# Both parts of a projection block behind one step of the recurrent heads, and none behind every second step

## The chip, the cores and the metric

The kernel runs on one core of one Trainium2 chip. The metric is the device time of one execution in microseconds; of the kernel before, three executions are given, and one more was profiled.

## The reference

A one-layer encoder trunk runs on two token groups with shared weights, a sample group of 1024 tokens and a prompt group of 512, both 1024 wide, in float32:

```python
h = rms_norm(x, norm_mix_g)
proj = h @ w_in                                  # 8 blocks of 512 columns
aq, ak, av, hq, hff, hfb, hi, hg = split(proj)
att = diff_attention(aq, ak, av)                 # 4 heads, softmax with a distance bias
q, v = silu(hq), hi                              # 4 recurrent heads, 128 x 128
f = lb + (1 - lb) * sigmoid(hff or hfb)          # a gate for each direction
o = hgrn2_scan(q, 1 - f, v, log f)  forwards  +  the same backwards
hgo = rms_norm(o, hg_norm_g) * silu(hg)
x = x + concat(att, hgo) @ w_out
x = x + expert_choice_ffn(rms_norm(x, norm_ffn_g))   # 16 experts
return rms_norm(x, final_norm_g)
```

Within the scan, token t reads token s through the product of all gates between them. The kernel works that out over levels of doubling length instead of token by token.

## The kernel before

The mixer (the first 940 us or so) runs the four recurrent heads of the sample, its four attention heads, and then the same for the prompt. The experts follow. The change lies in the recurrent heads.

**A recurrent head** (function `hgrn`, L843) takes tokens in blocks of 512: `NB` is 2 for the sample and 1 for the prompt. Its steps stand in the list `slots` (L884 to L893): `start`; `v_rows` for each block; for each block eight `level` steps and a `diag`; for each direction `k_rows` and `state` for each block; then `o`, `squares`, `mean`, `norm`, `mix`. Step names with numbers are written here as in the list: `("level", b, k)` is level k of block b, `("state", d, b)` is direction d, block b.

- A `level` step on TensorE is 64 small matmuls (L994; 32 at L1000 for level 6, 16 at L1005 for level 7) that read q and k of both directions. On VectorE it multiplies q and k by products of gates, three instructions a direction (L1134, L1135, L1137; one, L1127, at level 0). VectorE's update waits until TensorE has read (`level_read`, L1166), and TensorE's next level waits for the update (`updated`, L986).
- `diag` has nothing for TensorE. VectorE masks and reduces four banks of scores (L1177, L1182), and the next block's level 0, or `k_rows` and `state`, wait until the bank that they write has been read (`x_uses`, L899).
- `k_rows` is four transposes on TensorE (L1016) and a copy on ScalarE (L1105). `state` is four products on TensorE (L1025), then a chain of short additions on VectorE (L1195, L1198). `k_rows` (1,0) takes the bank that `state` (0,1) filled, and `o` (L1045) needs all states.

**The next head's projection** is computed beside the present head's steps (class `Projection`, L510). It has ten units (five outputs V, Q, two gates and G, each in two halves of the contraction), `NB` blocks for each unit, and each block in `CUTS` = 2 parts of six matmuls with 512 columns (L599 to L601). The method `piece` (L605) turns the number of a part into steps: the part itself, `("unit", u, b, part)`; ahead of a unit's first part the `split` of unit u + 1 (ScalarE L568 rounds the weights, VectorE L572 makes the remainder); behind the last part of an output its `land` (ScalarE L1075, and for Q and G VectorE L1150). A unit's first part waits for its own split's remainder (`lo`, L580).

**The order** is written out, not found by a scheduler. `beside` (L617) walks through the head's steps, counts them (all but `squares` and `mean`), and puts behind each step so many parts that their number keeps in proportion; `lead` parts, `NB` of them, go in at once. Every engine runs this one list in its own queue, skipping what isn't its own, and an instruction that waits holds up all behind it on that engine. The list is `stages[1]`. It is run for three heads of each group: a loop of two (`heads`, L735) and the one after it, in which the prompt has some extra steps for the output weights. The fourth head of each group runs without a projection beside it (`stages[2]`), mixed with the first attention projection. `beside` also makes `stages[0]`, which has a single step.

SyncE loads the raw weights (L556) into a ring of five slots. A load waits for the split five units earlier (L555).

Of the kernel before, what the change touches and what calls it, by code (L numbers as in the profile page):

```python
# [29 lines left out]
CUTS = 2  # L30
# [585 lines left out]

def beside(slots, proj, lead=0):  # L617


    pieces = CUTS * proj.units * proj.NB  # L620
    out, done, passed = [("split", 0)], 0, 0
    counted = lambda step: step[0] not in ("squares", "mean")
    total = sum(map(counted, slots))
    for step in slots:
        out.append(step)
        passed += counted(step)
        upto = lead + (pieces - lead) * passed // total
        for n in range(done, upto):
            out += proj.piece(n)
        done = upto  # L630
    return out
# [211 lines left out]
def hgrn(sem, g, T, w_in, masks_in, consts, banks, mem, after, rows):  # L843
# [47 lines left out]
    if NB == 2:  # L891
        slots += [("o", 1), ("norm", 0), ("squares", 1), ("mean", 1), ("mix", 0)]
    slots += [("norm", NB - 1), ("mix", NB - 1)]  # L893
    stages = beside([("none",)], proj), beside(slots, proj, NB), slots
    in_order = [s for s in slots if s[0] == "state"]
    nth = lambda step: in_order.index(step)
# [700 lines left out]
def project_out(sem, xs, w_out, g_ffn, w_router, consts, banks, mem, aff, aff_last, shares, index, index_cols, gate_cols, h2_dram, y_dram, rows, before_h, before):  # L1597
# [255 lines left out]
    def vector(dve):  # L1853
# [74 lines left out]
        return body  # L1928

    return Heads(None, (early, beside, tiles), (early_loads, late_loads), tensor, scalar, vector, gpsimd, {})  # L1930


def experts(nc, ctx, w_gate, w_up, w_down, g_final, ident, minus_half, psum, banks, index_cols, gate_cols, h2_dram, y_dram, out_p, out_s):
# [13 lines left out]
    with ExitStack() as c:  # L1947
# [74 lines left out]
        def pair_steps(i, late, last):  # L2022

            out = []
            after = {Q - 1: ("gate", 0), Q: ("silu", 0), 2 * Q - 1: ("up", 0), 2 * Q: ("high", 0), 2 * Q + 1: ("low", 0),
                     3 * Q - 1: ("gate", 1), 3 * Q: ("silu", 1), 4 * Q - 1: ("up", 1), 4 * Q: ("high", 1), 4 * Q + 1: ("low", 1)}
            for p in range(2):
                for n in range(UNITS):
                    ahead = n + PARTS - 1
                    if ahead < UNITS:  # L2030
                        out.append(("split", i, p, ahead))
                    elif not (last and p == 1):
                        out.append(("split", *next_of(i, p), ahead - UNITS))
                    out.append(("unit", i, p, n))
                    if n in after:
                        out.append((after[n][0], i, p, after[n][1]))
                    if n == 4 * Q + 2 and not (last and p == 1):
                        out.append(("turn", *next_of(i, p)))
                    if late:
                        u = (2 * i + p - FIRST_LATE) * UNITS + n  # L2040
                        out += [(kind, i, p, q) for later, kind in enumerate(("square", "mean", "norm")) for q in beside(u, later)]
                out.append(("last" if last and p == 1 else "result", i, p))
            return out
# [421 lines left out]
```

How the kernel before makes its waits and increments, by code:

```python
    def step(self, dve, n):  # L156
        rows, table, column, what = self.steps[n]
        eight, places = (t[rows, column:column + TOP] for t in (self.shares, self.index))
        if n:
            dve.wait_ge(self.sem, n)
        if what == 0:
            dve.max(eight, table).then_inc(self.sem, 1)
        elif what == 1:
            dve.max_index(places, eight, table).then_inc(self.sem, 1)
        else:
            dve.match_replace(table, eight, table, -2.0).then_inc(self.sem, 1)
# [59 lines left out]
    def halves(self, pool):  # L227
        pool.memset(self.minus_half[:], -0.5).then_inc(self.halved, 1)
        pool.wait_ge(self.halved, 1)
# [9 lines left out]
    def scalar(self, act):  # L239
        act.wait_ge(self.chain, 3)
        act.activation(self.lam_exp[:], self.lam_sum[:], ACT.Exp).then_inc(self.exps, 1)
        act.activation(self.lb_e[:], self.lb_r[:], ACT.Exp).then_inc(self.exps, 1)
        act.wait_ge(self.filled, self.FILLED)
# [4 lines left out]
    def vector(self, dve):  # L248
        chain, att_g, lb, lb_e, lb_r = self.chain, self.att_g, self.lb, self.lb_e, self.lb_r
        dve.wait_ge(self.loaded, 7 * 16)
        for n in range(2):
            dve.tensor_tensor_reduce(out=self.lam_prod[:, n, :], in0=self.lam_in[:, 2 * n, :],
                                     in1=self.lam_in[:, 2 * n + 1, :], scale=1.0, scalar=0.0,
# [9 lines left out]
        dve.wait_ge(chain, 5)  # L263
        dve.tensor_tensor(lb_e[:], lb_e[:], lb_r[:], ALU.mult).then_inc(chain, 1)
        dve.wait_ge(chain, 7)
```

## Time and profile before

| | us |
|---|---|
| three executions, median (lowest, highest) | 2191.89 (2191.11, 2194.22) |
| the profiled execution | 2191.68 |
| its span, first to last instruction | 2189.9 |
| TensorE matmuls busy | 2008.1 (92%) |
| VectorE busy | 1468.9 (67%) |
| ScalarE busy | 1111.4 (51%) |
| GpSimd busy | 290.1 (13%) |

By stage, the first three sample heads lie between about 87 and 348 us, and TensorE is busy 252.69 us of those 261; the first three prompt heads lie between about 756 and 895 us, with TensorE busy 128.28 of 139.

In a timeline row the first number is the start in us from the span's start and the second how long the instruction (or a merged run of `xN` of them) took. The end of a matmul overlaps the start of the next, so the step from start to start is what one costs. PE is TensorE, DVE VectorE, ACT ScalarE. A bracket gives the idle time of the engine in front of the instruction, and who ended it.

### The profile page before, as it was taken

The page shows a single profiled execution, that of the slowest core. Times are in us where ns is not written, and L with a number is a line of the kernel's source. Part 1 is how long each engine was busy: PE and PEld are TensorE (multiplying, and loading weights), DVE is VectorE, ACT ScalarE, POOL GpSimd, SP SyncE. Part 2 cuts the span into 40 slices and gives each one's busy share as a digit, 9 for nine tenths or more (in the row PEclk, how much of TensorE's full clock was granted, in tenths as well). Part 3 has the DMA queues.
Part 4 walks back from the last instruction along what each step waited for, and adds up shares of the span by engine and source line. Part 5 has one row for each costly group of instructions (what it writes and reads, how often), then busy time and mean ns, then how long its engine had stood idle before and what let it go on. Part 6 is the DMA issues. An engine that isn't in the chain of part 4 may idle for free. (4 is left out here: it accounts for less than half of the span.)

```text
span 2189.9 us, 43441 instructions
## 1 busy us (share of the span) xinstructions
PE 2008.1 (92%) x16048; PEld 1753.0 (80%) x16048; DVE 1468.9 (67%) x2769; ACT 1111.4 (51%) x1983; POOL 290.1 (13%) x419
## 2 busy tenths in 40 slices
PE   7999998899897899798899379999999999999996
PEld 6877876777786777676788279999999999999995
DVE  5466575666666577676348857777777777778876
ACT  5322322456565523265322156767666667667774
POOL 1101101000000011100122001111111111111234
PEclk9999998999998999999999689999999999999998
DMA  5211100100002122211233088787778787778995
GB/s 180 83 31 31 35 26 16 38 20 24 19 6 82 48 59 83 64 53 53 106 114 114 36 273 260 249 258 249 259 247 262 245 260 248 255 255 301 348 323 188
DMA packets 183465, 317.82 MB, mean 145 GB/s; under 512 B 11872, under 2 KB 82016, under 8 KB 183328
## 3 DMA queue, kind: packets, MB, share of 16 engines
q1 hardware_dynamic: 169984, 281.06, 38.1%
q0 software_dynamic: 8608, 30.68, 5.6%
q10 hardware_dynamic: 4736, 4.19, 0.6%
q8 instruction: 93, 1.52, 0.3%
q14 instruction: 44, 0.36, 0.1%
HBM read 279.97 MB, written 35.91 MB: 144 GB/s over the span
## 5 line engine op out<-in xcount | busy, mean ns | idle before, releaser
L2267 DVE TENSOR_TENSOR we_lo<-raw,we_hi 128x1024 fp32r<-128x1024 f32 x384 | 466.1, 1224 | 188.8 <-ACT we_hi L2192 187.8
L2158 PE MATMUL psum<-x_parts,we_hi 128*128 128x384 f32 x2048 | 585.0, 360 | 3.1 <-DVE we_lo L2267 3.1
L2160 PE MATMUL psum<-x_parts,we_lo 128*128 128x192 f32 x2048 | 513.4, 251 | 0.0
L2192 ACT CAST we_hi<-raw 128x1024 fp32r<-128x1024 f32 x384 | 400.1, 1054 | 156.6 <-PE psum L2160 93.3
L2160 PEld LDWEIGHTS psum<-x_parts,we_lo 128*128 128x128 f32 x2048 | 392.0, 191 | 0.6
L2158 PEld LDWEIGHTS psum<-x_parts,we_hi 128*128 128x128 f32 x2048 | 385.5, 188 | 4.1 <-issue 3.5
L599 PE MATMUL psum<-hT_hi,w_hi 128*128 128x512 f32 x512 | 215.5, 421 | 0.8 <-issue 0.8
L601 PE MATMUL psum<-hT_hi,w_lo 128*128 128x512 f32 x512 | 203.6, 398 | 0.0
L600 PE MATMUL psum<-hT_lo,w_hi 128*128 128x512 f32 x512 | 202.9, 396 | 0.0
L599 PE MATMUL psum<-hP_hi,w_hi 128*128 128x512 f32 x256 | 109.5, 428 | 15.9 <-DVE w_lo L572 11.6
L601 PEld LDWEIGHTS psum<-hT_hi,w_lo 128*128 128x128 f32 x512 | 97.8, 191 | 22.0
L599 PEld LDWEIGHTS psum<-hT_hi,w_hi 128*128 128x128 f32 x512 | 98.0, 191 | 20.2 <-issue 1.2
L600 PEld LDWEIGHTS psum<-hT_lo,w_hi 128*128 128x128 f32 x512 | 98.4, 192 | 16.6
L572 DVE TENSOR_TENSOR w_lo<-w_raw,w_hi 128x512 fp32r<-128x512 f32 x96 | 68.6, 715 | 52.3 <-ACT w_hi L568 50.1
L601 PE MATMUL psum<-hP_hi,w_lo 128*128 128x512 f32 x256 | 102.8, 401 | 0.0
L600 PE MATMUL psum<-hP_lo,w_hi 128*128 128x512 f32 x256 | 102.7, 401 | 0.0
L2174 PE MATMUL psum<-we_hi,hid_parts 128*128 128x512 f32 x256 | 101.3, 396 | 0.0
L568 ACT CAST w_hi<-w_raw 128x512 fp32r<-128x512 f32 x96 | 59.1, 616 | 80.9 <-PE psum L601 80.7
L2175 PE MATMUL psum<-we_lo,hid_parts 128*128 128x512 f32 x256 | 99.8, 390 | 0.0
L2176 PE MATMUL psum<-we_hi,hid_parts 128*128 128x512 f32 x256 | 99.7, 390 | 0.0
L2178 PE MATMUL psum<-we_lo,hid_parts 128*128 128x512 f32 x256 | 99.6, 389 | 0.0
L2177 PE MATMUL psum<-we_hi,hid_parts 128*128 128x512 f32 x256 | 99.6, 389 | 0.0
(313 smaller groups left out, 3774.0 us busy)
## 6 DMA issues: line engine op xcount, KB each, us to landing
raw<-in_w_gate SPq DMA_DIRECT2D x128, 512.0 KB, 4.7
raw<-in_w_up SPq DMA_DIRECT2D x128, 512.0 KB, 6.7
raw<-in_w_down SPq DMA_DIRECT2D x128, 512.0 KB, 5.0
w_raw<-in_w_in SPq DMA_DIRECT2D x96, 256.0 KB, 2.9
y_rows<-x SPq DMA_DIRECT2D x12, 512.0 KB, 2.6
h_rows<-h SPq DMA_DIRECT2D x12, 512.0 KB, 2.9
y<-y_rows SPq DMA_DIRECT2D x12, 512.0 KB, 7.9
w_raw_s<-in_w_in SPq DMA_DIRECT2D x16, 256.0 KB, 2.9
```

What stands on the lines that cost most here:

```text
L599: pe.matmul(out[:], mem.w_hi[:, u % 2, n, :], hi, start=(k == 0), stop=False)
L600: pe.matmul(out[:], mem.w_hi[:, u % 2, n, :], lo, start=False, stop=False)
L601: mm = pe.matmul(out[:], mem.w_lo[:, u % 2, n, :], hi, start=False, stop=(k == DT - 1))
L2158: pe.matmul(out[:, 0:2 * SLOTS], w_hi[:, s, at], x_parts[p][:, k, :, :], start=(k == 0), stop=False, skip_group_check=True)
L2160: mm = pe.matmul(out[:, SLOTS:2 * SLOTS], w_lo[:, s, at], x_hi[p][:, k, :], start=False, stop=(k == DT - 1), skip_group_check=True)
L2174: pe.matmul(out[2 + h][:], a, u, start=first, stop=False)
L2175: pe.matmul(out[2 + h][:], a, v, start=False, stop=False)
L2176: pe.matmul(out[2 + h][:], b, u, start=False, stop=last)
L2177: pe.matmul(out[h][:], both, u, start=first, stop=False)
L2178: mm = pe.matmul(out[h][:], both, v, start=False, stop=last)
L2192: act.copy(w_hi[:, n % PARTS, :], raw[:, s, :]).then_inc(hi.sem, 1)
L2267: dve.tensor_tensor(w_lo[:, n % PARTS, :], raw[:, n % RAW, :], w_hi[:, n % PARTS, :].bitcast(F32), ALU.subtract).then_inc(lo.sem, 1)
```

## The change

Before parts are put behind a step, the number reached is rounded down to an even number, so that both parts of a block stand behind the same step. The last step still reaches all parts. A sample head's first step gets two parts, where it had three; a prompt head's keeps two.

```diff
 def beside(slots, proj, lead=0):
 
-
     pieces = CUTS * proj.units * proj.NB
     out, done, passed = [("split", 0)], 0, 0
     counted = lambda step: step[0] not in ("squares", "mean")
     total = sum(map(counted, slots))
     for step in slots:
         out.append(step)
         passed += counted(step)
         upto = lead + (pieces - lead) * passed // total
+        upto -= upto % CUTS
         for n in range(done, upto):
             out += proj.piece(n)
         done = upto
     return out
```

For steps that follow each other in a sample head this gives (sN is the split of unit N, u.b.p part p of block b of unit u):

```
step            before             after
level 0, 3      s3 2.0.0           -
level 0, 4      2.0.1              s3 2.0.0 2.0.1
level 0, 5      2.1.0              -
level 0, 6      2.1.1              2.1.0 2.1.1
level 0, 7      s4 3.0.0           -
diag 0          3.0.1 3.1.0        s4 3.0.0 3.0.1
level 1, 0      3.1.1 land Q       3.1.0 3.1.1 land Q
```

and in a prompt head:

```
step            before             after
level 0, 6      4.0.1              s5 4.0.0 4.0.1
level 0, 7      s6 5.0.0           -
diag 0          5.0.1 land         s6 5.0.0 5.0.1 land
k_rows 0, 0     s7 6.0.0           -
state 0, 0      6.0.1              s7 6.0.0 6.0.1
k_rows 1, 0     s8 7.0.0           -
state 1, 0      7.0.1 land         s8 7.0.0 7.0.1 land
```

## Rows read from the trace of the kernel before

**Rows 1.** Busy time by stretch: window, length, busy us of each engine, granted clock (PEclk)
```profile
core 0: us, PE busy (x) PEld busy (x) DVE busy (x) ACT busy (x) POOL busy (x), PEclk, DMA share, GB/s
87.00:174.00 87.00, 83.67 (x1215) 66.36 (x1214) 55.82 (x140) 23.05 (x57) 10.93 (x24) 1.00 0.11 33
203.00:210.00 7.00, 5.18 (x138) 3.56 (x137) 5.91 (x10) 1.10 (x2) 2.35 (x8) 0.79 0.09 27
```
**Rows 2.** Timeline of TensorE, sample head, block 0: level 3, a part, level 4
```profile
102.41 0.76 PE L994 MATMUL psum<-q,k 128*32 128x32 f32 x64
103.12 0.48 PE L599 MATMUL psum<-hT_hi,w_hi 128*128 128x512 f32 x1
...
104.69 0.76 PE L994 MATMUL psum<-q,k 128*32 128x32 f32 x64
```
**Rows 3.** Timeline of VectorE: first and last instruction of updates, level 3 and level 1
```profile
102.95 0.22 DVE L1134 TENSOR_TENSOR fup<-fup 128x64 f32<-128x64 f32 x1 [0.55 <-PE psum L994]
...
104.23 0.42 DVE L1137 TENSOR_TENSOR k<-k,fup 128x256 f32<-128x256 f32 x1
...
185.25 0.42 DVE L1134 TENSOR_TENSOR fup<-f 128x256 f32<-128x256 f32 x1 [1.02 <-PE psum L994]
...
186.94 0.42 DVE L1137 TENSOR_TENSOR k<-k,f 128x256 f32<-128x256 f32 x1
```
**Rows 4.** Timeline: a level that waited for the update, block 1, level 2
```profile
124.46 0.41 DVE L1137 TENSOR_TENSOR k<-k,f 128x256 f32<-128x256 f32 x1
124.92 0.46 PE L994 MATMUL psum<-q,k 128*32 128x32 f32 x32 [0.55 <-DVE k L1137]
125.31 0.50 PE L599 MATMUL psum<-hT_hi,w_hi 128*128 128x512 f32 x1
```
**Rows 5.** Timeline: level 7 and diagonal of block 0, three parts, level 0 of block 1
```profile
111.38 0.97 PE L1005 MATMUL psum<-q,k 128*64 128x64 f32 x16
112.28 0.50 PE L599 MATMUL psum<-hT_hi,w_hi 128*128 128x512 f32 x1
...
113.60 0.68 DVE L572 TENSOR_TENSOR w_lo<-w_raw_s,w_hi 128x512 fp32r<-128x512 f32 x1
...
116.60 0.33 PE L994 MATMUL psum<-q,k 128*32 128x32 f32 x16
...
118.65 0.55 DVE L1177 TENSOR_TENSOR table<-psum,table 128x384 f32<-128x384 f32 x1
...
119.76 0.50 PE L599 MATMUL psum<-hT_hi,w_hi 128*128 128x512 f32 x1
```
**Rows 6.** Timeline: k_rows (1,0), k_rows (1,1), state (1,0), o of the same head
```profile
148.19 1.11 DVE L1198 SCALAR_TENSOR_TENSOR state<-state,fend_f,psum 128x128 f32<-128x128 f32 x3 [2.30 <-PE psum L1025]
149.37 0.66 PE L1016 MATMUL psum<-ident,k 128*128 128x128 f32 x4
...
151.25 0.60 PE L1016 MATMUL psum<-ident,k 128*128 128x128 f32 x4
151.89 0.59 ACT L1105 COPY k_rows<-psum 128x512 f32<-128x512 f32 x1 [1.24 <-PE psum L1016]
...
155.35 1.05 PE L1025 MATMUL psum<-v_rows,k_rows 128*128 128x128 f32 x8
156.44 1.12 DVE L1198 SCALAR_TENSOR_TENSOR state<-state,fend_b,psum 128x128 f32<-128x128 f32 x3 [0.82 <-PE psum L1025]
...
157.81 0.46 PE L1045 MATMUL psum<-v_rows,at 128*128 128x128 f32 x2
```
**Rows 7.** Timeline of a prompt head: levels 5 and 6, k_rows (0,0), o
```profile
818.44 0.76 PE L994 MATMUL psum<-q_p,k_p 128*32 128x32 f32 x64
...
821.81 0.50 PE L599 MATMUL psum<-hP_hi,w_hi 128*128 128x512 f32 x1
...
827.15 0.60 PE L1016 MATMUL psum<-ident,k_p 128*128 128x128 f32 x4
...
831.72 0.68 DVE L572 TENSOR_TENSOR w_lo<-w_raw,w_hi 128x512 fp32r<-128x512 f32 x1
...
836.22 0.45 PE L1045 MATMUL psum<-v_rows,at_p 128*128 128x128 f32 x2
```

## The prediction

> **What bounds the kernel now.** I read the busy shares by stage first, then the timeline of TensorE through one recurrent head, then VectorE over the same stretch. In the first of the changed heads TensorE is busy 83.67 of 87.00 us at full clock, VectorE 55.82 and ScalarE 23.05 [rows 1]. So the head costs what TensorE issues, plus its few gaps, and the question is which gaps a new order opens.
>
> Inside the head a chain runs under that busy engine. A level's score matmuls on TensorE must read q and k before VectorE may update them, and the next level's matmuls need the update: TensorE level k, VectorE update k, TensorE level k+1. What hides the update is the projection part between two levels. A level takes 103.12 - 102.41 = 0.71 us to issue, a part with its entry and exit 104.69 - 103.12 = 1.57, so levels follow each other every 2.28 us [rows 2]. A longer group of parts costs less per part: three take 116.60 - 112.28 = 4.32, so each part beyond the first costs (4.32 - 1.57)/2 = 1.38 and two together 2.95 [rows 2, 5]. An update of both directions lasts from 102.95 to 104.23 + 0.42 = 104.65, thus 1.70 us, starting 0.54 after the level's start [rows 2, 3]; at level 1, whose products are wider, 186.94 + 0.42 - 185.25 = 2.11 [rows 3]. The signal to TensorE takes 124.92 - (124.46 + 0.41) = 0.05 us, say 0.06, and the second direction of a level then takes 125.31 - 124.92 = 0.39 [rows 4].
>
> **The change, part by part.** Nothing is added or removed; parts move. Rounding `upto` down to a whole block holds every first part back one step, where it meets its second. The 1024-token pass has 35 counted steps with 40 parts, the 512-token pass 18 with 20. Working the list out by hand: after the change no parts stand after levels 1, 3, 5 and 7 of either block, after v_rows 1, k_rows (0,0) and (1,1), state (0,1) and (1,0), o 1 and mix 0; in the 512-token pass after v_rows, levels 1, 3, 5, 7, both k_rows, and o. The list serves three heads of each pass (a loop of two and the one after it). The steps "split" and "land" move with the parts.
>
> *Level pairs, 1024 tokens.* With nothing between them, the second level's second direction can start 0.54 + 1.70 + 0.06 = 2.30 after the first level's start, ends 0.39 later, and two parts follow: 2.30 + 0.39 + 2.95 = 5.64 us for two levels and two parts, now 2 x 2.28 = 4.56. That is +1.08 each for levels 3-4 and 5-6 of both blocks: +4.3. Levels 1-2 of block 0 use the 2.11 update: +1.5.
>
> *Block 0's diagonal to level 2 of block 1.* Level 7 starts at 111.38, the masked products hold the score banks until 118.65 + 0.55 = 119.20, and parts resume at 119.76 [rows 5]; level 2's next part starts at 125.31 [rows 4] and ends at 126.88, six parts in all. After the change the split on VectorE at 113.60, which holds the diagonal back by 0.60 (its 0.68 overlaps the next), stands behind it. So banks come free 0.60 earlier, parts resume at 119.16 and two end at 122.11. Level 1's update started at 124.87 - 2.11 = 122.76 because VectorE first waited for a landing of the part just ended, 1.40 after level 1's start (119.76 + 1.60 = 121.36). The same 1.40 again gives 123.51, + 2.11 + 0.06 + 0.39 = 126.07, + 2.95 = 129.02: +2.1. It also takes 1-2 of block 1 in.
>
> *State steps.* k_rows (1,0) starts at 149.37, just after VectorE's state chain ends at 148.19 + 1.11 = 149.30; so does o 0 at 157.81, after 156.44 + 1.12 = 157.56 [rows 6]. These starts are set by VectorE and don't move when the part in front of them goes; the part is owed behind them: +1.4 each, +2.8. Between k_rows (1,1) at 151.25 and its state step ScalarE's copy must end (151.89 + 0.59 + 0.06 = 152.54, 1.29 after) where a part now covers it; then state 0.81 and two parts 2.86 make 4.95, against 155.35 - 151.25 = 4.10: +0.85 [rows 6]. The 0.81 is an estimate of the state step's issue, its row's 1.05 less the overlap of its end, and 2.86 is the pair's 2.95 less the dearer exit to a level.
>
> *Head entry, k_rows (0,0), end of head.* One part fewer stands before level 0, which waits for GpSimd's k; the part follows behind. No row here shows that margin. The norm chain at the end has as many parts around it as before. I take -0.2 for group entries saved (1.57 - 1.38 = 0.19 each); bounds -1 (five entries) and +2 (the moved part wholly exposed, and some of the norm).
>
> Sum for a 1024-token head: 1.5 + 4.3 + 2.1 + 2.8 + 0.85 - 0.2 = 11.4 us; three heads, 34.
>
> *512 tokens.* Levels 1-2 +1.5, levels 3-4 +1.1. At 5-6 the landing of Q delays the update today: level 5 starts at 818.44 and parts resume at 821.81, 3.37 later [rows 7]. That wait stays, with 2.95 behind it in place of 1.57: +1.4. The largest term is the diagonal. Split 6 moves behind it on VectorE, and unit 6 is the next one TensorE wants, after the state step. Today the split that follows the diagonal is number 7, at 831.72 to 832.40; with split 6 taken from in front, its place is 0.60 earlier, so unit 6 can start at 831.86. TensorE has finished the state step at 827.15 + 1.29 + 0.81 = 829.25, so it stands 2.6 us. Then two parts to 834.8, ScalarE's copy until 1.29 after its start (k_rows (1,0), 834.8 to 836.1), state 0.81, two parts 2.86: o starts at 839.8, now 836.22; k_rows (0,0) is at 827.15 in both [rows 7]. That is +3.6. At the end of the head split 9 now follows the norm: +0.3. Sum 1.5 + 1.1 + 1.4 + 3.6 + 0.3 - 0.1 = 7.8; three heads, 23.
>
> *Loads.* SyncE's queue keeps its order; each load waits for a split that comes at most one step later, and the ring is five slots deep. I take nothing; bounds 0 and +1 us per head.
>
> *Clock.* The granted clock was 0.79 over 203 to 210 us, in the second head, where TensorE was busy 5.18 of 7.00; over the first head's same place it stayed at 1.00 [rows 1]. That is 0.21 x 7 = 1.5 us lost after one stall. The three new 2.6 us stalls of the 512-token diagonal look like it; I take two falls, +3, with bounds 0 and +33 (below).
> The Trainium skill, "TensorE: Matmul & The Clock Gate", section "A second HAM failure mode: psum-queue depth-cycling", tells of a kernel whose short idles between groups of matmuls made the clock swing between its two levels. By that rule all the small gaps here count, not the long ones alone; the trace has it after the long gap of the diagonal and not in the first head.
>
> Total 34 + 23 + 3 = 60 us. The profiled execution took 2191.68 us (span 2189.9), the median of three runs is 2191.89, so the two can be used alike: 2191.7 + 60 = 2252 us.
>
> **Rivals.**
> *A: fewer changes of group win (faster, 2182 us).* Runs of parts fall from 31 to 20 in a 1024-token head and from 16 to 10 in a 512-token one, 51 in all; each saves 1.57 - 1.38 = 0.19 us, 9.7 us. It needs the empty steps to cost nothing: a level's update would have to be done within the level's own 0.71 us. Against it: 1.70 us [rows 3]. It decides from the point where update plus signals is under 0.9 us.
> *B: no change (2192 us).* Waits shift onto stalls that exist anyway. For it: VectorE is idle a third of the head. Against: it is idle waiting for TensorE, and TensorE has 3.3 us of gaps in 87 [rows 1].
> *C: levels pay, the rest is hidden (2221 us).* If the state and diagonal terms are absorbed, there remain 3 x (1.5 + 4.3) + 3 x (1.5 + 1.1 + 1.4) = 29 us. For it: these terms rest on an order of several engines. Against: VectorE sets those starts today [rows 6, 7].
> *D: the clock falls often (2282 us).* There are 45 new gaps (ten and five per head); if half bring the 1.5 us of the second head, +33 less the 3 counted. The skill's rule above is this case. Against: the level pairs keep TensorE busy about four fifths.
>
> **Numbers.** Forecast 0.74, A 0.02, B 0.03, C 0.11, D 0.10. The forecast's own range is 2236 to 2268 (entries, loads, sizes of waits). Taking in most of C and D gives 2220 to 2282. A change of 0.2%, about 4 us, is what a measurement of this kernel can tell from none. Faster 0.02, same 0.03, slower 0.95.
>
> **What would show it.** TensorE's idle before the matmuls of even levels should be about 1.3 us a time, released by VectorE's update of k, with none before odd levels. In the 512-token heads the first matmul of unit 6 should wait about 2.6 us for w_lo, and state steps should wait for ScalarE's k_rows. A 1024-token head should last about 98 us, a 512-token one 52 to 53. It would be wrong if TensorE's idle between two levels without parts is under 0.5 us, or if heads keep their length while another stage moves.

## The result, and the profile after

The changed kernel took 2265.11 us (median of three, 2261.26 to 2267.69) against 2191.89. The ratio is 1.0329, 95% interval 1.0314 to 1.0345. The forecast was 2252 us within 2220 to 2282. The profiled execution took 2261.26 us, span 2259.5.

First the page of the changed kernel, its busy times:

```profile
PE 2023.2 (90%) x16048; PEld 1768.3 (78%) x16048; DVE 1466.4 (65%) x2769; ACT 1110.4 (49%) x1983; POOL 292.5 (13%) x419
```

The instruction counts are those of before. TensorE is busy 15.1 us longer with the same matmuls: part of it ran at half clock. The rest of the 69.6 us that the span grew, 54.5, is time in which TensorE waits. Next the busy time of the two changed stages, from the first transpose of `v_rows` of head one to that of head four, first of the kernel before:

```profile
core 0: us, PE busy (x) PEld busy (x) DVE busy (x) ACT busy (x) POOL busy (x), PEclk, DMA share, GB/s
91.59:346.88 255.29, 247.50 (x3619) 196.79 (x3618) 163.52 (x417) 64.78 (x164) 31.15 (x71) 0.99 0.11 31
760.10:891.21 131.11, 123.12 (x1802) 96.08 (x1801) 92.09 (x224) 43.14 (x101) 15.98 (x39) 1.00 0.23 67
```

and of the changed kernel:

```profile
core 0: us, PE busy (x) PEld busy (x) DVE busy (x) ACT busy (x) POOL busy (x), PEclk, DMA share, GB/s
89.14:383.39 294.25, 253.69 (x3625) 204.57 (x3624) 163.49 (x418) 64.56 (x165) 33.45 (x72) 0.98 0.09 27
799.09:961.15 162.06, 132.90 (x1801) 104.38 (x1800) 91.21 (x224) 43.10 (x101) 15.98 (x39) 0.94 0.18 54
```

The three sample heads take 39.0 us more, the three prompt heads 31.0, the whole span 69.6. What stands ahead of them is 2.5 us shorter and the fourth sample head 2.4 longer, which cancel; no other stage differs by more than 0.4. In the prompt heads the mean clock fell from 1.00 to 0.94, 0.06 x 162 = 9.7 us, and TensorE's busy time rose by as much (9.8).

Inside a head, the timeline of TensorE in the second sample head of the changed kernel answers to [rows 2, 4]: levels 1, 2 and 3, then 4 and 5.

```profile
194.10 0.76 PE L994 MATMUL psum<-q,k 128*32 128x32 f32 x64
195.79 0.46 PE L994 MATMUL psum<-q,k 128*32 128x32 f32 x32 [0.93 <-DVE k L1137]
196.80 0.46 PE L994 MATMUL psum<-q,k 128*32 128x32 f32 x32 [0.55 <-DVE k L1137]
...
200.14 0.76 PE L994 MATMUL psum<-q,k 128*32 128x32 f32 x64
201.62 0.46 PE L994 MATMUL psum<-q,k 128*32 128x32 f32 x32 [0.72 <-DVE k L1137]
202.43 0.46 PE L994 MATMUL psum<-q,k 128*32 128x32 f32 x32 [0.35 <-DVE k L1137]
...
205.80 0.76 PE L994 MATMUL psum<-q,k 128*32 128x32 f32 x64
```

Each even level waits twice for VectorE's update of k, once for each direction, and odd levels not at all. Levels 1 and 2 with their pair of parts take 200.14 - 194.10 = 6.04 us, levels 3 and 4 take 5.66; the prediction had 0.54 + 2.11 + 0.06 + 0.39 + 2.95 = 6.05 and 5.64. The waits of all changed heads together say the same. Of TensorE from 89 us to 962 us in the changed kernel (what it waited for: us in total, times, longest):

```profile
PE psum L994 <- DVE k L1137: 20.3, 30, 1.7
PE psum L599 <- DVE w_lo L572: 15.5, 4, 8.7
...
PE psum L994 <- DVE k_p L1137: 7.6, 12, 0.9
PE psum L1025 <- ACT k_rows L1105: 6.7, 9, 0.9
PE psum L1000 <- DVE k L1137: 6.5, 14, 0.8
...
PE psum L1016 <- DVE state L1198: 5.9, 4, 2.0
PE psum L1000 <- DVE k_p L1137: 5.4, 6, 1.6
PE psum L1045 <- DVE state L1198: 4.9, 4, 1.4
```

and in the same stages of the kernel before, 89 to 892 us:

```profile
PE psum L599 <- DVE w_lo L572: 10.5, 4, 8.7
...
PE psum L994 <- DVE k L1137: 4.0, 9, 0.7
...
PE psum L1016 <- DVE state L1198: 2.0, 1, 2.0
...
PE psum L1045 <- DVE state L1198: 0.9, 1, 0.9
...
PE psum L1000 <- DVE k L1137: 0.6, 2, 0.4
PE psum L1000 <- DVE k_p L1137: 0.5, 2, 0.3
PE psum L994 <- DVE k_p L1137: 0.3, 1, 0.3
```

The waits for k rise from 5.4 us to 39.8, for the state chain from 2.9 to 10.8, for the weights' remainder (`w_lo`) from 10.5 to 15.5, and the 6.7 us for ScalarE's `k_rows` copy are new. Together that is 54.0 us, nearly all of the 54.5. (One wait of 8.7 us for `w_lo` stands in both kernels.) The state steps of the second sample head, in the timeline of the changed kernel, answer to [rows 6]:

```profile
254.69 0.66 PE L1016 MATMUL psum<-ident,k 128*128 128x128 f32 x4 [1.29 <-DVE state L1198]
...
257.95 0.60 PE L1016 MATMUL psum<-ident,k 128*128 128x128 f32 x4
259.22 1.16 PE L1025 MATMUL psum<-v_rows,k_rows 128*128 128x128 f32 x8 [0.68 <-ACT k_rows L1105]
...
262.97 1.05 PE L1025 MATMUL psum<-v_rows,k_rows 128*128 128x128 f32 x8
265.43 0.46 PE L1045 MATMUL psum<-v_rows,at 128*128 128x128 f32 x2 [1.41 <-DVE state L1198]
```

The wait for a state chain was covered by a part before and is now bare. In the second prompt head, `k_rows` (0,0), unit 6 and `o` answer to [rows 7]:

```profile
881.96 0.60 PE L1016 MATMUL psum<-ident,k_p 128*128 128x128 f32 x4
883.48 1.15 PE L1025 MATMUL psum<-v_rows,k_rows 128*128 128x128 f32 x8 [0.92 <-ACT k_rows L1105]
886.61 0.49 PE L599 MATMUL psum<-hP_hi,w_hi 128*128 128x512 f32 x1 [1.98 <-DVE w_lo L572]
887.40 0.41 PE L599 MATMUL psum<-hP_hi,w_hi 128*128 128x512 f32 x1
888.46 0.63 PE L599 MATMUL psum<-hP_hi,w_hi 128*128 128x512 f32 x1
...
891.02 0.62 PE L1016 MATMUL psum<-ident,k_p 128*128 128x128 f32 x4
...
896.15 0.38 PE L1045 MATMUL psum<-v_rows,at_p 128*128 128x128 f32 x2
```

Unit 6 waits for its weights' remainder, whose split now stands behind the diagonal. The matmul of 128x512 that takes 0.63 us, where others take some 0.4, is one at half clock, inside the pair that follows that stall: the pair lasts 891.02 - 886.61 = 4.41 us in place of 2.95.

### The profile page after: what moved, and what is told of

It is laid out like the page before. It is cut to its first block and busy times, and to the rows that moved or that the text cites. A ratio compares the mean times of both kernels' runs of the same rounds, so it can differ in the third digit from the quotient of the medians.

```text
span 2259.5 us, 43441 instructions
## 1 busy us (share of the span) xinstructions
PE 2023.2 (90%) x16048; PEld 1768.3 (78%) x16048; DVE 1466.4 (65%) x2769; ACT 1110.4 (49%) x1983; POOL 292.5 (13%) x419
## 5 line engine op out<-in xcount | busy, mean ns | idle before, releaser
L1075 ACT ACTIVATE land<-psum 128x512 f32<-128x512 f32 x60 | 35.9, 598 | 135.1 <-PE psum L601 135.0
```

## Experiments

The kernels are told in the order of the questions. "Changed" below means the kernel after the change. Medians are given; the kernel before was timed beside each group and had 2190.7, 2191.6 and 2191.0 us.

**Which heads.** Two kernels pair the parts in one group's heads only.

```diff
-        upto -= upto % CUTS
+        upto -= upto % CUTS if proj.NB == 2 else 0     # sample only; == 1: prompt only
```

> Parts are paired in the three sample heads alone; the prompt heads keep the order of before. My theory (new waits inside each group's own heads, plus falls of the clock after long stalls): the first sample v_rows of head four stood 36.5 us later in the changed kernel, so the time is 2192 + 36 = 2228 us, and TensorE's falls in the prompt heads are gone. Rival (the two groups share a cause, such as loads or a later stage that shifts): the sum of this run's and the prompt-only run's excess differs from 73 us by more than 8.

> Parts are paired in the three prompt heads alone. Theory: 31 to 34 us more than before, 2223 to 2226 us, of which some 9 is the half clock after the stall at the diagonal and elsewhere. Rival (my sum without the clock): 23 us more, 2215.

Sample only: 2229.27 us, ratio 1.018 (1.016 to 1.020). Prompt only: 2224.09 us, ratio 1.0150 (1.0133 to 1.0167). Over 2190.7 that is 38.6 and 33.4, together 72.0, against 73.2 of the change itself. Each group's heads keep the length and clock of the kernel before when only the other group is changed: the prompt heads of the first take 131.07 us at clock 1.00, the sample heads of the second 254.38 at 0.99. So nothing shared, such as the loads, carries the loss. The prompt's 33 is also well over the 23 of my sum without the clock.

**The place of the splits.** Only the matmul parts are paired; a split stays behind the step where it was.

```diff
+        if len(slots) > 1:
+            for n in range(ahead, upto):
+                out += [of for of in proj.piece(n) if of[0] == "split"]
+            ahead = upto
         upto -= upto % CUTS
         for n in range(done, upto):
-            out += proj.piece(n)
+            out += [of for of in proj.piece(n) if of[0] != "split" or len(slots) == 1]
```

> The changed kernel, but each split stays behind the step where it stood before; only matmul parts are paired. Theory: the prompt's unit 6 no longer waits for a split behind the diagonal. A prompt head then reaches o about 0.9 us later than before instead of 3.6, and saves 0.3 at its end: 3 x 3.0 = 9 us less, some 3 more for a stall after which the clock fell; a sample head's diagonal starts 0.6 later, 2 us back. 2265 - 10 = 2255 us. Rival (the place of the parts is all that counts): 2265 us.

2251.01 us, 14 below the changed kernel where 10 were expected. Its two stages:

```profile
90.06:386.21 296.15, 253.69 (x3625) 204.93 (x3624) 162.72 (x418) 64.92 (x165) 32.52 (x72) 0.98 0.09 27
800.88:947.70 146.82, 123.86 (x1801) 98.69 (x1800) 91.88 (x224) 43.09 (x101) 14.63 (x39) 0.99 0.21 60
```

The sample heads take 1.9 us more than in the changed kernel, as expected (their diagonal starts a split later). The prompt heads take 15.2 less, and their clock is back to 0.99. About 9 of the 15 was expected of the wait of unit 6; the rest goes with the clock, taken up next. What remains is 146.8 - 131.1 = 15.7 us, of which 0.01 x 147 = 1.5 is clock: 14.2 us or 4.7 a head. By the prediction's terms the levels and the bare `k_rows` copy make 1.5 + 1.1 + 1.4 + 0.9 = 4.9.

**The clock.** The changed kernel gets extra 128x512 matmuls into a bank that nobody reads at that time; they stand in TensorE's new waits. Their results are not used.

```diff
+            of_head(step, i, j)                       # the step itself, as before
+            many = {"level": 3 if step[0] == "level" and step[2] in (1, 3, 5) else 0,
+                    "k_rows": 2 if NB == 1 or step[1:] == (1, 1) else 0,
+                    "state": 6 if NB == 1 and step[1:] == (0, 0) else 0}.get(step[0], 0)
+            if many and j is not None:                # the next kernel: and NB == 1
+                pe.wait_ge(v_rows.sem, v_rows.last(i))
+                for _ in range(many):
+                    pe.matmul(TURN[:], mem.hT_hi[:, 0, 0:P], mem.hT_hi[:, 0, 0:BLK], start=True, stop=True)
```

> The changed kernel with extra matmuls of 128x512 into a bank that nobody reads then, placed where TensorE stands idle: 3 after levels 1, 3, 5, 2 after the exposed k_rows, 6 after the prompt's state (0,0). They add 0.7 us to 1.3 us gaps and lie inside the waits. Theory (about 13 us of the loss is half clock after idle stretches): with the engine busier the granted clock in the prompt heads rises from 0.94 towards 1.00 and the time falls by 5 to 12 us, to 2253 to 2260, although 120 matmuls and more are added. Rival (the gaps alone are the loss, the clock falls by itself): 2265 to 2270 us and the same number of falls.

2246.68 us: 18 below the changed kernel, beyond the 5 to 12 expected. But the changed kernel itself was timed on another occasion. So it was timed again, beside one filled in the prompt heads only.

> The changed kernel itself, timed beside the next two. Theory: 2261 to 2268 us as before. Rival (part of the 18 us between it and the filled one was another chip or day): nearer 2257.

> The changed kernel with the extra matmuls in the prompt heads only. In the first filled kernel the three prompt heads took 153.2 us against 162.1 in the changed one, with no fall of the clock in place of six, and the sample heads 292.1 against 294.3. Theory (half clock costs where TensorE sets the pace, and in the prompt heads it does after each stall): nearly all the gain stands, 8 to 11 us less than the changed kernel in this call. Rival (the gain lay in later stages, by how falls happen to lie there): less than 4 us, with shorter prompt heads paid back later.

Changed again: 2258.79 us (2254.54 to 2267.23), below the range expected and near the rival's 2257. Filled in the prompt only: 2250.28, 8.5 less, as expected (8 to 11). The prompt stage of three kernels, in order the changed one repeated, filled in both groups, and filled in the prompt only:

```profile
795.93:953.66 157.73, 128.56 (x1801) 101.27 (x1800) 91.15 (x224) 43.11 (x101) 17.13 (x42) 0.97 0.19 56
```
```profile
796.62:949.85 153.23, 138.61 (x1859) 106.80 (x1858) 91.40 (x224) 43.12 (x101) 15.97 (x39) 1.00 0.19 57
```
```profile
797.95:951.18 153.23, 138.62 (x1859) 106.80 (x1857) 91.41 (x224) 43.22 (x101) 15.97 (x39) 1.00 0.19 57
```

At clock 1.00, 0.97 and 0.94 the three heads take 153.2, 157.7 and 162.1 us: each 0.03 of clock is 4.5 us, which is 0.03 x 155 = 4.7. The first number, with 58 matmuls added (x1859 against x1801), is what the prompt heads cost by waits alone: 22.1 us over before. The other 9 of the 31 were half clock.

A "fall" below is a stretch of matmuls at half clock. The profile of the changed kernel has six in the prompt heads and its repeat three, each some 3.4 us long, which makes (162.1 - 153.2)/6 and (157.7 - 153.2)/3 = 1.5 us a fall in both. Two of the six follow the long stall at unit 6, in the second and third head; the other four follow level pairs, whose two waits make only 1.5 to 1.8 us. The same waits in other heads brought none, and the count differs between two executions of one program. Of the 18 us, part was therefore scatter of the first timing; 8 to 12 is the clock's.

The sample heads allow the same reading. Four profiles have them with the same list of steps and no filling (us, with the granted clock):

| kernel | first head | second | third | sum |
|---|---|---|---|---|
| changed | 97.46 (1.00) | 98.46 (0.98) | 98.33 (0.95) | 294.25 |
| changed again | 97.24 (1.00) | 98.54 (0.98) | 96.83 (0.96) | 292.61 |
| filled in the prompt only | 99.04 (0.98) | 98.32 (0.98) | 95.54 (0.98) | 292.90 |
| sample only | 97.49 (1.00) | 98.38 (0.98) | 95.50 (0.98) | 291.37 |

In the first and third column a head is 1.3 to 1.6 us longer for each fall. The changed kernel has one in its second head and three in its third (two of them end to end), thus some 6 us of the sample's 39. Filling saved little of that (292.1 us in the kernel filled in both groups), for two falls, one of them double length, came all the same.

**Which steps.** Parts are paired behind level steps alone.

```diff
-        upto -= upto % CUTS
+        upto -= upto % CUTS if step[0] == "level" else 0
```

> Parts are paired behind the level steps alone; start, v_rows, diag and all steps behind them have the parts of before (what a level held back comes at the next such step). Theory, by my terms: a sample head loses 1.5 + 4.3 + 1.2 (the last for block 1's levels 1-2, whose landing still waits for a part), 7.0 us; a prompt head 4.0 for its levels and 3.4 because split 6 stands behind the diagonal here too; 3 x 14.4 = 43 us, and 5 to 9 for falls of the clock: 2239 to 2243 us. Rival (the state steps, with their chains on VectorE and ScalarE, carry most of it): under 2225 us.

2246.49 us, ratio 1.0257 (1.0241 to 1.0273), 3.5 over the expected range. The stages:

```profile
91.89:366.91 275.02, 246.66 (x3619) 198.83 (x3618) 162.28 (x417) 64.78 (x164) 32.20 (x71) 0.99 0.10 29
781.38:942.83 161.45, 131.18 (x1802) 103.98 (x1801) 92.13 (x224) 43.12 (x101) 16.04 (x39) 0.93 0.18 54
```

The sample heads lose 19.7 us or 6.6 a head (expected 7.0), so the levels are half of the sample's loss. By the prediction's terms the state steps (3.65 a head) are most of the rest; no run has them alone. The prompt heads lose 30.3, of which 0.07 x 161 = 11 is clock and 19 waits (expected 22). Nearly the whole prompt loss is there without the state steps being touched, because the late split 6 comes with the level pairing.

**The other way: a part moved into a wait.** [Rows 5] shows the wait at the diagonal of block 0, where the kernel before has three parts. Here the sample heads' parts ahead of that diagonal come one later, so that four stand there and one fewer ahead of level 0.

```diff
+    held = lambda step: ("diag", 0) in slots and slots.index(step) < slots.index(("diag", 0))
...
-        upto = lead + (pieces - lead) * passed // total
+        upto = lead + (pieces - lead) * passed // total - (proj.NB == 2 and held(step))
```

> The kernel before, with the sample heads' parts ahead of the first diagonal one step late: start has two parts in place of three, and the diagonal of block 0 has three in place of two, where TensorE waits some 3 us for the score banks. Theory: level 0 comes one part earlier and everything up to the diagonal with it, and the part is given back where TensorE stands: 1.4 to 1.6 us a head, 4 to 5 us, 2186 to 2187 us. Rival (VectorE, not TensorE, sets the head's pace up to level 2 of block 1, so an earlier start is lost there): 2191 us.

2182.37 us (2180.50 to 2186.49), ratio 0.9965 (0.9955 to 0.9975): faster than both kernels, and below the 2186 to 2187 expected. Its sample stage and, in the timeline, the diagonal of its first head:

```profile
90.30:340.03 249.73, 245.96 (x3625) 195.92 (x3624) 164.67 (x418) 65.57 (x165) 33.51 (x72) 1.00 0.11 32
```
```profile
110.06 0.97 PE L1006 MATMUL psum<-q,k 128*64 128x64 f32 x16
110.96 0.50 PE L599 MATMUL psum<-hT_hi,w_hi 128*128 128x512 f32 x1
...
116.63 1.03 PE L995 MATMUL psum<-q,k 128*32 128x32 f32 x64
117.59 0.50 PE L599 MATMUL psum<-hT_hi,w_hi 128*128 128x512 f32 x1
```

Level 0 of block 1 now runs through without a bracket, and the three heads take 5.6 us less (expected 4 to 5). The profiled execution, at 2185.68, was one of the slower.

The edit moves more than a part. With the parts, split 4 goes from behind level 7 to behind the diagonal, and on VectorE the last read of a score bank ends 6.96 us after level 7's start (116.46 + 0.56 - 110.06) where it was 7.82 (119.20 - 111.38). Of TensorE's gain here, 1.38 us is the part that fits into the wait, and 0.85 (level 7 to the next part: 8.38 before, 7.53 now, with one part more) goes with the earlier banks. No run has the one without the other.

Holding two parts (`2 * (...)`) was tried too:

> As the kernel with one part held, but two: start has one part, the first diagonal four. Theory: level 0 can come another part earlier, until GpSimd's k, which ended 1.4 us before it: 1 to 1.4 us a head more, 2178 to 2180 us. Rival (TensorE then waits for k at level 0, or the wait at the diagonal was already filled): 2182 to 2184 us.

2184.77 us, ratio 0.9974 (0.9963 to 0.9984), no better, and a little above the rival's 2184. The wait at the diagonal was already filled: in the first head level 0 of block 1 starts 117.39 - 109.43 = 7.96 us after level 7, where it was 116.63 - 110.06 = 6.57 with one part held, later by the whole of the fifth part. The timeline shows another wait in front, of the second `v_rows` for ScalarE's copy:

```profile
91.34 0.66 PE L976 MATMUL psum<-ident,land 128*128 128x128 f32 x4 [0.39 <-ACT v_rows L1088]
```

**Filling waits of the kernel before.** The extra matmuls again, now in the kernel before and in the one with a part held.

`idle(bank, n)` issues n of the 128x512 matmuls of the filled kernels. `j` is None in the fourth heads, so these get 24 (sample) or 14 (prompt) around level 0; every sample head gets nine at level 0 of block 1.

```diff
+            if j is None and step == ("v_rows", 1):
+                pe.wait_ge(*x_uses[3].before(i, ("level", 0, 0)))
+                idle(X[3], 10)
+            if j is None and step == ("level", 0, 0):
+                pe.wait_ge(v_rows.sem, v_rows.last(i))
+                idle(TURN, 8)                          # and 6 behind this step
...
                         if k == 0 and d == 0:
+                            if b and n:
+                                idle(TURN, 3)
                             pe.wait_ge(*x_uses[n].before(i, step))
```

> The kernel before with extra 128x512 matmuls in TensorE's waits: 9 in block 1's level 0 of every sample head, and 24 (sample) or 14 (prompt) around level 0 of the fourth heads. Theory (the clock falls after waits of a few us, and those falls cost 1.7 us for each 3.4): the falls after 206, 292, 350, 377 and 896 us go, 27 us at half speed, up to 13 us less, 2 or 3 added: 2180 to 2184 us. Rival (falls come anyway, or the work added costs what it saves): 2189 to 2196 us.

> Both of the last two: one part held to the diagonal, and the waits filled. Theory: the gains nearly add, since the part takes 1.4 us of the wait and the fill the rest; some of the fill then delays level 0 of block 1, about 0.5 us a head: 2178 to 2182 us. Rival: no better than the better of the two.

2193.29 us, ratio 1.0015 (1.0006 to 1.0024), and 2192.70, ratio 1.0005 (0.9995 to 1.0015). The theory failed: no gain, and in the second all of the held part's gain was lost. In the first, the falls in the first three sample heads are gone (clock 1.00), yet the heads are as long as before:

```profile
90.65:346.16 255.51, 252.73 (x3646) 199.52 (x3645) 163.89 (x417) 64.77 (x164) 31.65 (x71) 1.00 0.11 31
```

255.51 against 255.29 us. By heads it is 87.25, 86.25 and 82.01 against 86.95, 86.22 and 82.12. The first head had no fall before, and there the filling cost 0.3 us; the second and third had one each, and lost and gained 0.1 at most. So the fall after the diagonal in [rows 1] was worth no more than about 0.4 us. The likely reason is that level 2 waits for VectorE some 0.8 us where no fall comes, and without a bracket after the fall. My price for it, 1.5 us, was read from the clock alone. In the kernel with a part held, the same stage is:

```profile
90.01:347.01 257.00, 254.07 (x3653) 200.67 (x3651) 164.82 (x418) 65.57 (x165) 31.08 (x72) 1.00 0.11 31
```

257.00 against 249.73 us without the fill. There the held part had already used up the wait at the diagonal, and the nine extra matmuls a head stand on TensorE's path: with them, level 0 of block 1 takes 3.8 us in the first head, where it took 1.0. That is 7.3 us over three heads, most of the 10.3 that this kernel loses. The fourth sample head got 1.4 us shorter by the filling of the first kernel (88.57 against 89.97), with no gain in the whole; why not stays open.

## Why the prediction was right, and by how much it was off

The direction, the mechanism and the range held. The waits came out at some 54 us for 57 said and the clock at 15 for 3, errors that partly cancel. By the prediction's own steps:

- *Level pairs.* Right to 0.02 us each where shown; released by VectorE's update of k, as said.
- *Diagonal to level 2.* In the second sample head of the changed kernel level 7 starts at 211.36 and level 3 of block 1 at 230.07, 18.7 us. A pair there ran at half clock (4.42 us in place of 2.95), so 17.2 is left. The prediction has 129.02 - 111.38 = 17.6.
- *State steps.* `k_rows` (1,0) and `o` waited 1.29 and 1.41 us for the state chain, the state step 0.68 for ScalarE. From `k_rows` (1,0) to `k_rows` (1,1) it is 257.95 - 254.69 = 3.26, before 1.88, thus +1.38 as said.
- *Sample sum.* Said 11.4 a head, 34. Measured 39.0 over the stage, of which 1.4 is one part that now stands behind its first transpose and not before it, and some 6 the clock (four falls at 1.3 to 1.6 us; the two of the kernel before cost next to nothing). About 32 remain, so the waits were put 2 too high, of which 0.4 in the head above lies between the diagonal and level 2; the rest isn't traced to a step.
- *Prompt sum.* Said 7.8 a head, 23. With the clock at 1.00 it is 22.1. From `k_rows` (0,0) to `o` it took 14.2 us; less the 1.5 of half clock 12.7, as said (839.8 - 827.15). The wait for the split, said to be 2.6, was 1.98, but it ended on time: unit 6 starts 4.65 us after `k_rows` (0,0), said 4.71. I counted the wait from the issue of the state step (0.81), the bracket from its end (1.15), and the step in front started 0.23 later, behind the copy.
- *Clock.* This is the term that was mis-sized: said 3 us, measured 9 in the prompt heads and some 6 in the sample heads, 15 in all, which is also what TensorE is busy longer. The price of a fall, 1.5 us, fits the changed heads; but I took it from a place where a fall cost at most 0.4, so that it fits is partly luck. Wrong was the number of falls. The two falls that I took after the long stalls came. Four more in the prompt heads follow short gaps: in the second, matmuls at half clock follow levels 1-2 and 5-6, whose waits are 1.5 and 1.8 us (862 and 875 us in the timeline). The sample heads, for which I took none, have four. So the short gaps count as well.
- *Length of heads.* A sample head lasts 98.1 us on average (said 98). A prompt head lasts 54.0 with the falls and 51.1 without them (said 52 to 53).

The Trainium skill, "TensorE: Matmul & The Clock Gate", section "A second HAM failure mode: psum-queue depth-cycling", says that frequent short idles between groups of matmuls can make the clock swing. The trace agrees in the prompt heads (0.94 against 1.00), but rival D's size did not come: 45 new gaps brought ten falls and not 22.

Rival A (fewer group changes win) was wrong by its own condition, as was B. C, that only the levels pay, is ruled out for the sample heads by the levels-only kernel (6.6 us a head of 13), and for the prompt heads by the one whose splits stay (15.2 us less with the same level pairs).

## What to carry to other kernels

Where one engine's filler work hides another engine's reply, what counts is the size of each filler, not their sum: two portions behind every second step leave one reply bare and cover the next twice. Price such a change gap by gap from the timeline, then look which weight preparation moves behind a long block on its own engine. A stall of TensorE costs a second time through the clock only where TensorE also sets the pace afterwards, so read the length of the stage, not the granted clock, before paying for filler.

## What the runs showed of the hardware

Adding matmuls made a kernel faster: with 58 more of 128x512 in the three prompt heads, the stage went from 162.1 and 157.7 us to 153.2, at a granted clock of 0.94, 0.97 and 1.00 (full speed, 2.4 GHz, being 1.00). The falls in the changed heads follow stretches in which TensorE waited 1.5 to 3.5 us between matmuls, yet stretches of the same kind in other heads brought none: the profile has six falls in the prompt heads, its repeat three. A fall lasted some 3.4 us and cost 1.5 us where TensorE set the pace. In the kernel before, where the next level waits for VectorE, it cost at most 0.4, and there the same remedy gained nothing.
